# Seven half-width block products in the second FFN, with GpSimd making the operand sums

## The reference, cut to what matters

```python
def swiglu(h, w_gate, w_up, w_down):
    return (jax.nn.silu(h @ w_gate) * (h @ w_up)) @ w_down

x = x + g2 * swiglu(modulate(x, norm_ffn_g[l], sh2, sc2), ffn_w_gate[l], ffn_w_up[l], ffn_w_down[l])
```

## Time and profile before

| | |
|---|---|
| time, median of 3 | 1623.81 us (1623.81 to 1623.95) |
| the profiled execution | 1622.71 us |
| its span | 1620.9 us |
| TensorE busy | 1583.2 us, 98% |
| VectorE busy | 991.5 us, 61% |
| ScalarE busy | 647.5 us, 40% |
| GpSimd busy | 133.7 us, 8% |

### The profile page before, as it was taken

How to read it: one execution, slowest core, us unless ns; L and a number is a source line. 1 busy time by engine, 2 the same in 40 slices (tenths; PEclk the granted TensorE clock), 3 DMA queues, 4 the chain that set the end, 5 groups by cost and what they waited for, 6 DMA issues and landing times.

```text
span 1620.9 us, 25828 instructions
## 1 busy us (share of the span) xinstructions
PE 1583.2 (98%) x10032; PEld 1362.1 (84%) x10032; DVE 991.5 (61%) x1547; ACT 647.5 (40%) x1187; POOL 133.7 (8%) x183
## 2 busy tenths in 40 slices
PE   6999999999999999999999999999999999999999
PEld 5887777678799899899989977888887888888887
DVE  4798888543896388368638666877665533333334
ACT  4444454442743144124214343556683322322222
POOL 0434353010000000000000100100110000000000
PEclk9999999999999999999999999999999999999999
DMA  9633400651113321422231431111135233232332
GB/s 366 73 98 105 144 27 27 231 212 65 66 53 120 115 77 48 164 77 79 104 132 63 149 105 53 53 40 40 66 136 184 78 108 117 91 128 92 116 105 104
DMA packets 49491, 170.48 MB, mean 105 GB/s; under 512 B 5584, under 2 KB 5840, under 8 KB 49264
## 3 DMA queue, kind: packets, MB, share of 16 engines
q1 hardware_dynamic: 37104, 127.00, 22.9%
q10 hardware_dynamic: 7984, 28.31, 4.9%
q0 software_dynamic: 4304, 13.80, 2.9%
HBM read 164.87 MB, written 4.19 MB: 104 GB/s over the span
## 4 chain that ended last, share of the span: by engine, by line
PE 91%; DVE 4%; ACT 3%; issue 1%; DMA 0%; ACTq 0%; SPq 0%; DVEq 0%
PE PS L711 39%; PE PS L2776 9%; PE PS L2557 8%; PE PS L2400 6%; PE PS L2404 6%; PE PS L2401 6%; PE PS L2511 1%; PE PS L2471 1%; PE PS L2362 1%; DVE c_early L1868 1%; PE PS L2624 1%; PE PS L2862 1%; PE PS L2605 1%; PE PS L2863 1%; PE PS L2523 1%
## 5 line engine op out<-in xcount | busy, mean ns | idle before, releaser
L675 DVE TENSOR_TENSOR w_lo<-raw,w_hi 128x1024 fp32r<-128x1024 f32 (+2 forms) x172 | 192.2, 1117 | 128.4 <-ACT w_hi L669 125.2
L669 ACT ACTIVATE w_hi<-raw 128x1024 fp32r<-128x1024 f32 (+2 forms) x172 | 165.4, 962 | 221.4 <-PE PS L711 156.9
L711 PE MATMUL PS<-c_hi,w_hi 128*128 128x512 f32 (+1 forms) x672 | 203.4, 357 | 1.0 <-DVE c_lo L1585 0.6
L711 PE MATMUL PS<-c_lo,w_hi 128*128 128x512 f32 (+1 forms) x672 | 202.0, 354 | 0.0
L1560 DVE SCALAR_TENSOR_TENSOR X<-PS,mod,X 128x512 f32<-128x512 f32 (+2 forms) x120 | 75.7, 658 | 198.2 <-PE PS L711 191.8
L711 PE MATMUL PS<-c_hi,w_lo 128*128 128x512 f32 (+1 forms) x672 | 152.0, 355 | 0.0
L711 PE MATMUL PS<-h_hi,w_hi 128*128 128x512 f32 x368 | 139.2, 385 | 0.9 <-ACT scr L903 0.6
L711 PE MATMUL PS<-h_lo,w_hi 128*128 128x512 f32 x368 | 139.0, 385 | 0.0
L1868 DVE SCALAR_TENSOR_TENSOR c_early<-X,small,c_early 128x798 f32<-128x798 f32 x120 | 134.0, 1116 | 2.9
L711 PEld LDWEIGHTS PS<-c_hi,w_hi 128*128 128x128 f32 x672 | 110.7, 188 | 21.0 <-issue 1.2
L711 PEld LDWEIGHTS PS<-c_lo,w_hi 128*128 128x128 f32 x672 | 110.4, 188 | 18.6
(11 more groups left out here) (405 smaller groups left out, 3080.1 us busy)
## 6 DMA issues: line engine op xcount, KB each, us to landing
raw<-in_w SPq DMA_DIRECT2D x152, 512.0 KB, 3.3
adaw<-in_ada ACTq DMA_DIRECT2D x28, 512.0 KB, 4.3
adaw<-in_w SPq DMA_DIRECT2D x20, 512.0 KB, 4.1
scr<-in_ada POOLq DMA_DIRECT2D x19, 512.0 KB, 9.1
raw<-in_w SPq DMA_DIRECT2D x24, 384.0 KB, 3.1
h_early<-in_ada SPq DMA_DIRECT2D x12, 512.0 KB, 6.2
scr<-in_ada ACTq DMA_DIRECT2D x12, 512.0 KB, 6.8
scr<-in_ada SPq DMA_DIRECT2D x4, 1024.0 KB, 14.3
```

What stands on the lines that cost most here:

```text
L669: nc.scalar.activation(w_hi[:, j, 0:tiles], raw[:, j].rearrange("p (k n) -> p k n", k=KT)[:, 0:tiles], ACT.Copy).then_inc(s_hi, 1)
L675: nc.vector.tensor_tensor(w_lo[:, j, 0:tiles], raw[:, j].rearrange("p (k n) -> p k n", k=KT)[:, 0:tiles], w_hi[:, j, 0:tiles].bitcast(f32) ...
L711: last = nc.tensor.matmul(G[j][:, a:b], w[:, j, k], m[:, k, a:b], start=(n == 1), stop=(n == 3 * k_tiles))
```

## The change

Of the second FFN's 22 gate/up pairs, 20 are now made by seven block products of 12 matmuls with 256 columns each, 84 in place of 48 with 512. The numbers 1 to 7 name the products. Four points differ from the first FFN:

- **Chained PSUM.** A pair uses three banks. 1, 6, 7 and 4 add up in one bank, 5 and 3 in the second, 2 has the third. Before 6 is added, ScalarE copies 1 out (`copied_1`); before 7, the sum so far (`copied_u2`); before 3, product 5 (`copied_5`). VectorE reads the bank after 7 (`up_1`) before 4 is added. Two pairs alternate between banks 0 to 2 and 5 to 7.
- **Seven weight slots.** Each product has its own slot for `hi` and `lo` (two lie in unused columns of `c_hi` and `c_lo`).
- **GpSimd** makes the four sums of a pair's weights (four 128x512 operations, called op 1 to op 4 here) and one of the four sums of inputs. Op 3 overwrites the block of product 1 and so waits for its `lo`.
- **Order.** TensorE takes 1, 5, then 4 of the pair before, then 6, 3, 2, 7. At a group's end the first down slice begins before product 4 of the last pair and goes on after it.

During the norm ScalarE also writes `h_whole` (8 more operations of 128x512). SyncE loads a pair's two 128x1024 chunks into `raw` or `adaw` in turn. The first FFN and all else stay as they were.

GpSimd's list:

```diff
+            for q in range(NB, 2 * NB):
+                a0, a1, u0, u1 = (four(chunk(q, c)[:, n:n + 512]) for c in range(2) for n in (0, 512))
+                for c in range(2):
+                    pool.wait_ge(s_pw[q % 2][c], 16 * (q // 2) + 16)
+                if q >= NB + 2:
+                    pool.wait_ge(s_bl, 7 * (q - 2) + SPLIT_AT[7])
+                nc.gpsimd.tensor_tensor(SUM_7[q % 2], a0, u0, ALU.subtract).then_inc(s_sb, 1)
+                pool.wait_ge(s_sb, 4 * q + 1)
+                nc.gpsimd.tensor_tensor(u0, u0, u1, ALU.add).then_inc(s_sb, 1)
+                pool.wait_ge(s_sb, 4 * q + 2)
+                pool.wait_ge(s_bl, 7 * q + SPLIT_AT[1])
+                nc.gpsimd.tensor_tensor(a0, u0, a0, ALU.subtract).then_inc(s_sb, 1)
+                pool.wait_ge(s_sb, 4 * q + 3)
+                if q >= NB + 2:
+                    pool.wait_ge(s_bl, 7 * (q - 2) + SPLIT_AT[3])
+                nc.gpsimd.tensor_tensor(SUM_3[q % 2], a1, a0, ALU.subtract).then_inc(s_sb, 1)
```

ScalarE's, for the pairs of a group:

```diff
+                    for q in range(first, end):
+                        last = q + 1 == end
+                        copied_1(q)
+                        stream_hi(act, q, 6)
+                        copied_5(q)
+                        stream_hi(act, q, 3)
+                        if q == NB:
+                            act.wait_ge(s_gf[1], half + 1)
+                            hidden_hi(1)
+                            sum_hi(3)
+                        stream_hi(act, q, 2)
+                        copied_u2(q)
+                        stream_hi(act, q, 7)
+                        if q > first:
+                            pair_hi(q - 1, q - 1 + tile)
+                        stream_hi(act, q, 4)
+                        silu_1(q)
+                        if not last:
+                            stream_hi(act, q + 1, 1)
+                        else:
+                            act.wait_ge(s_bp, BLOCK_AT[q, 5])
+                            split_hi(act, R // 2, 0, tiles=nf)
+                        silu_0(q)
+                        if not last:
+                            stream_hi(act, q + 1, 5)
+                    pair_hi(q, q + tile)
```

VectorE's:

```diff
+                    for q in range(first, end):
+                        last = q + 1 == end
+                        if q > first:
+                            up_1(q - 1)
+                            gated_1(q - 1)
+                        stream_lo(dve, q, 6)
+                        stream_lo(dve, q, 3)
+                        if q == NB:
+                            hidden_lo(1, 1)
+                            sum_lo(2)
+                        if q > first:
+                            gated_0(q - 1)
+                        stream_lo(dve, q, 2)
+                        stream_lo(dve, q, 7)
+                        if q > first:
+                            hidden_lo(q - 1 + tile, q - 1 + tile - f0)
+                        stream_lo(dve, q, 4)
+                        gate_1(q)
+                        if q == NB:
+                            sum_lo(3)
+                        if not last:
+                            stream_lo(dve, q + 1, 1)
+                        else:
+                            split_lo(dve, R // 2, 0, tiles=nf)
+                        gate_0(q)
+                        if not last:
+                            stream_lo(dve, q + 1, 5)
+                    up_1(q)
+                    gated_1(q)
+                    gated_0(q)
+                    hidden_lo(q + tile, q + tile - f0)
```

TensorE's (a bank's product also waits for the bank's readers, which is cut here):

```diff
+            def stream_block(q, b):
+                pe.wait_ge(s_bh, 7 * q + SPLIT_AT[b])
...
+                for k in range(4):
+                    MM(chained(q, b), w_h[:, k], m_h[:, k], start=(opens and k == 0), stop=False, skip_group_check=not opens)
+                    MM(chained(q, b), w_h[:, k], m_l[:, k], start=False, stop=False, skip_group_check=not opens)
+                pe.wait_ge(s_bl, 7 * q + SPLIT_AT[b])
+                for k in range(4):
+                    last = MM(chained(q, b), w_l[:, k], m_h[:, k], start=False, stop=(k == 3), skip_group_check=not opens)
+                last.then_inc(s_bp, 1)
...
+                for g, (f0, nf) in enumerate(GROUPS):
-                    with pe.Fori(1 if g == 0 else 0, nf) as i:
-                        half = pe.snap(i + R // 2)
-                        product(pe, half, 0, h_hi, h_lo, ONLY)
-                        product(pe, half, 1, h_hi, h_lo, ONLY)
+                    for q in range(first, end):
+                        stream_block(q, 1)
+                        stream_block(q, 5)
+                        if q > first:
+                            stream_block(q - 1, 4)
+                        for b in (6, 3, 2, 7):
+                            stream_block(q, b)
...
+                    pe.wait_ge(s_hid, hid - 1)
+                    for k in range(nf - 1):
+                        down_pass(k, w_hi, c_hi, nf)
+                        down_pass(k, w_hi, c_lo, nf)
+                    stream_block(end - 1, 4)
+                    pe.wait_ge(s_lo, R + 1)
+                    for k in range(nf - 1):
+                        down_pass(k, w_lo, c_hi, nf)
+                    pe.wait_ge(s_hid, hid)
+                    down_pass(nf - 1, w_hi, c_hi, nf)
+                    down_pass(nf - 1, w_hi, c_lo, nf)
+                    down_pass(nf - 1, w_lo, c_hi, nf).then_inc(s_gemm, 1)
```

More of the change, by code:

```diff
@@ L49, with block_stream @@
 R_F1 = R_O1 + 8
-NP = R_F1 + 2 * FT + 32
-NR = NP + 2 * (FT - PLAIN)
+NP = R_F1 + 2 * PLAIN + 32
+NB = FT - PLAIN
+NR = NP + 4 * NB
+def block_stream():
+    at, n = {}, 7 * NB
+    for f, end in zip(FIRST, PAIRS):
+        for q in range(NB + f, NB + end):
+            for b in (1, 5, 4, 6, 3, 2, 7):
+                if b != 4 or q > NB + f:
+                    n += 1
+                    at[q - (b == 4), b] = n
+        n += 1
+        at[NB + end - 1, 4] = n
+    return at
+BLOCK_AT = block_stream()
+SPLIT_AT = {1: 1, 5: 2, 6: 3, 3: 4, 2: 5, 7: 6, 4: 7}
 SM = {}
@@ L1003, in ffn, with gate_silu @@
             def ffn():
-                R = R_F1
-                def hidden(half, i):
+                R, half = R_F1, R_F1 // 2 + 1
+                def gate_silu(half):
                     act.wait_ge(s_gemm, 2 * half + 1)
@@ L1010, in hidden, with hidden_hi @@
                     nc.scalar.activation(sg[:, 0:LAT], G[0][:, 0:LAT], ACT.Silu).then_inc(s_gf[0], 1)
[L1011 to L1014, removed]
[L1016 to L1023 removed]
+                def hidden_hi(at):
+                    nc.scalar.activation(c_hi[:, at, 0:LAT], ftmp[:, 0:LAT], ACT.Copy).then_inc(s_hhi, 1)
@@ new lines, in silu_1, with pair_hi @@
+                def silu_1(q):
+                    act.wait_ge(s_g1s, q + 1)
+                    nc.scalar.activation(sg[:, LH:LAT], sg[:, LH:LAT], ACT.Silu).then_inc(s_s1, 1)
+                def pair_hi(q, at):
+                    act.wait_ge(s_f, 2 * q + 2)
+                    hidden_hi(at)
+                split_hi(act, half, 0)
+                act.wait_ge(s_nwh, 24)
+                gate_silu(half - 1)
+                act.wait_ge(s_gf[1], half)
+                hidden_hi(0)
+                split_hi(act, half, 1)
@@ new lines, in ffn @@
+                sum_hi(0)
+                gate_silu(half)
+                stream_hi(act, NB, 1)
+                sum_hi(1)
+                stream_hi(act, NB, 5)
+                sum_hi(2)
+                R += 2 * PLAIN
+                for g, (f0, nf) in enumerate(GROUPS):
+                    first, end = NB + FIRST[g], NB + PAIRS[g]
+                    tile = PLAIN - f0 - NB
+                    for q in range(first, end):
[17 more added lines that the diff above has]
+                            stream_hi(act, q + 1, 1)
+                        else:
+                            act.wait_ge(s_bp, BLOCK_AT[q, 5])
+                            split_hi(act, R // 2, 0, tiles=nf)
[3 more added lines that the diff above has]
+                    pair_hi(q, q + tile)
+                    act.wait_ge(s_bp, BLOCK_AT[q, 2])
@@ L1766, in hidden, with hidden_lo @@
                     V.tensor_tensor(ftmp[:, 0:LAT], G[1][:, 0:LAT], sg[:, 0:LAT], ALU.mult).then_inc(s_gf[1], 1)
[L1767 to L1770, removed]
-                dve.wait_ge(s_mod, 28)
-                for g, (f0, nf) in enumerate(GROUPS):
[L1774 to L1781, removed]
+                def hidden_lo(f, at):
+                    dve.wait_ge(s_hhi, FT + f + 1)
+                    V.tensor_tensor(c_lo[:, at, 0:LAT], ftmp[:, 0:LAT], c_hi[:, at, 0:LAT].bitcast(f32), ALU.subtract)\
+                        .then_inc(s_hid, 1)
```

221 lines of the change are left out of this document (196 added, 25 removed).

## The result

| | before | after |
|---|---|---|
| median of 5 runs | 1623.95 us (1623.81 to 1624.57) | 1642.27 us (1639.72 to 1644.74) |
| ratio, 95% interval | 1 | 1.0113 [1.0102, 1.0124] |
| profiled execution, its span | 1622.71, 1620.9 us | 1643.15, 1641.3 us |

What follows compares the result with a forecast made beforehand. TensorE's matmul time was taken to bound the second FFN. Groups 211.3, products 4 5.8, groups' ends 6.0 and start 1.5 make 224.6, minus 217.8 removed: 6.8 more than 1623.8, so 1630.6 us, range 1617 to 1637.

Steps and rivals of the forecast that it cites:

- Removed work: Second FFN, TensorE: 20 pairs of 48 matmuls at 0.2269 us go away, 217.8 us.
- the product's price: TensorE: matmuls of 256 columns start 0.12 us apart, so a block takes 1.44 us and a pair 10.08.
- The loop: Steady pair: block 5 waits for hi 5, behind silu_0, which waits for gate_0 behind lo 1; 10.84 us a pair.
- the forecast's own sign: TensorE's waits should fall on block 5; if block 1 waits instead, the loop's bound was misplaced.
- The shared port: GpSimd's sums and VectorE's SBUF operations take turns, each meeting costing VectorE 0.84 us; 11.25 a pair, bounds 10.84 and 11.37.
- that branch: Steady pair: lo 5 comes before op 4, later sums meet lo 6, lo 3 and lo 2; 11.14 us a pair.
- The first stretches: Each group, start to block 6 of its second pair: ten blocks, 14.4 us, plus about 0.35 for collisions.
- The groups' ends: Down stage: waits for the last hidden tile, 0.9 us and a restart, 1.3 in the last group; 6.0 together.
- The signs: TensorE's second-FFN waits rise to about 25 us, mostly block 5's hi and lo; met lo splits read 1.3 to 1.6.
- TensorE the bound: Rival, second FFN: TensorE stays the bound, 10.2 us less, 1613.6; with half of it near 1619; chance 0.20 for both.
- The loop alone: Rival, second FFN: the loop without port collisions, 10.84 us a pair, 1624.4 us, no change; chance 0.22.
- a second operation of GpSimd falls on the loop: Rival, steady pair: op 1 and op 2 reach lo 7 to lo 4; about 11.8 us a pair, 1638; chance 0.08.

Runs made afterwards that it cites:

- e4: The changed kernel with the four GpSimd weight sums moved to VectorE, hi 1 ahead of silu_1 and hi 5 ahead of silu_0: 1611.2 us, ratio 0.9917.
- e1: The changed kernel with each of GpSimd's four weight sums cut to 128x8 elements, order and semaphores kept: 1624.0 us, ratio 0.9992 to the kernel before.
- e7: e4 with the passes for c_lo that stood ahead of product 4 at group ends moved behind it: 1608.4 us, ratio 0.9906 to the kernel before.
- e3: The changed kernel with GpSimd's four sums cut to 128x8 elements, hi 5 ahead of silu_0 and lo 5 ahead of gate_0: 1614.3 us, ratio 0.9936.
- e2: The changed kernel with hi 5 ahead of silu_0 on ScalarE and lo 5 ahead of gate_0 on VectorE, sums whole: 1632.3 us, ratio 1.0047.
- e9: e4 with the weight sums back on GpSimd, its order of hi 1, hi 5 and the silus kept: 1620.1 us, ratio 0.9976 to the kernel before.
- e5: The changed kernel with op 1 and op 2 cut to 128x8 elements, op 3 and op 4 whole: 1624.9 us, ratio 0.9994 to the kernel before.

## Why the prediction was wrong, step by step

- **Removed work, and the product's price.** Right. Blocks lie 0.12 us a matmul apart, and with nothing to wait for (e4) a pair takes 10.00 us where 10.08 stood. By the Trainium skill ("TensorE: Matmul & The Clock Gate", section "Wait — 56ns, not 53.3ns?") it would be 9.2, an estimate from its 0.109 us a matmul. The trace of e4, where TensorE doesn't wait in a steady pair, shows 10.0.
- **The loop.** Right: block 5 behind hi 5 behind `silu_0` behind `gate_0`, block 1 to block 5 in 2.03 us (2.03 forecast), 10.80 a pair with the sums out of the way (10.84 forecast). The extended durations held: 0.42, 0.42, 0.39. By the forecast's own sign, a wait at block 1, the bound of the changed kernel was misplaced all the same; the next point says how.
- **The shared port: the step that failed.** The mechanism was right. The failed sentences are "op 4 and the next pair's op 1 and op 2 slide into the stretch of lo 6, lo 3 and lo 2, and lo 7 starts some 0.3 late: 11.14" and, in the sum, 11.25. Lo 5 did come first, as that branch has it, by 0.17 us (1410.53 against op 4 at 1410.70), with lo 5 0.8 later than worked out and op 4 1.1: that this branch came true is partly luck. Two sizes were off. The operations were costed at 1.02 each from a pair in which one operand is a single value per partition, spread over the row (L607); on two whole tensors one takes 1.29 alone and 1.48 to 1.68 in a collision, so the row of four lasts 6.2 us. And three VectorE instructions in a row are held up, by 0.57 + 1.09 + 1.09 = 2.75 us, against a slack of 1.91 (e1), where the forecast priced a meeting at 0.84 and never added up the three. Lo 7 was late by 0.8, not 0.3, and the bound moved off TensorE: a pair is then a loop of VectorE and ScalarE alone, 11.64. Twelve loops: 3.8 us.
- **The first stretches: the same error, twice as dear.** "About 0.35 for the same collision (0 to 0.65)" measured 2.0 (16.44 against 14.45 in e1, three times), and 2.9 in the first group (18.91 against 16.01), some 0.5 of which is the lower clock of the last section: block 5 began at 1296.55 though its hi was ready at 1295.97. At a group's start GpSimd does two pairs' sums in a row, from 1361.35 on in the trace, and meets lo 6, lo 3 and lo 2 with op 4, op 1 and op 2, as the first rows of the two timelines show. Blocks 6, 3 and 2 wait 0.18 each for their low halves, blocks 1 and 5 of the second pair 0.5 each, and each of the five has a restart of 0.1: 2.0 together. This and the first group's extra are 7.7 us of the 11.1 that were missing. I looked at the first stretch with the steady pair's eyes, though op 1 and op 2 of two pairs fall together there.
- **The groups' ends.** Right: waits of 3.4 us for `c_lo`, the longest 1.2 (forecast 0.9 three times and 1.3).
- **The signs.** TensorE's waits came to some 18 us, not 25, none of them for the `lo` of block 5, and met splits read up to 1.78 us where 1.3 to 1.6 was foretold.
- **Rivals.** TensorE the bound: e4 and e7 show what it would have taken, other lists and sums off GpSimd; even e3 stands at 10.20. The loop alone is what e1 shows. The rival "a second operation of GpSimd falls on the loop" (0.08, 11.8 a pair, 1638) was nearest, with one difference: op 1 and op 2 needn't reach lo 7 themselves; what they push in front of it is enough. Its condition, operations on two whole tensors costing well over 1.02, had been written down and put aside for the cheaper row.

The Trainium skill ("SBUF — State Buffer", section "Who interferes with whom") says that a VectorE instruction with two SBUF inputs contends with a GpSimd one that reads SBUF, and calls the shared port pair an exclusive lock. The traces agree: a VectorE instruction caught in a meeting ends 0.55 (512 columns) or 0.28 (256) behind GpSimd's, each time.

## What to carry to other kernels

When an idle engine takes over work, cost what it does to the engine that shares a resource with it before what it spares it: count the meetings in the order in which they come, add up what all of them cost it, and only then take off its slack ahead of the first instruction on the critical loop. Do it again for the first round of each loop, where the helper has several rounds' work at once. And in lists that run in order, put what the bounding engine waits for ahead of what merely waits for that engine: two entries moved were worth 0.6 us a pair, and made lateness elsewhere cheap.

## What the runs showed of the hardware

- GpSimd's 128x512 subtraction or addition on two whole tensors takes 1.29 us alone; with one operand spread from a single value per partition, two take 2.04. A row of the same size and another operand layout was not a fair price.
- VectorE's 128x512 split in a collision took 1.11 to 1.82 us for 0.69 (all traces here), and GpSimd's operation 1.47 to 1.78, once 2.16, for 1.29 (the changed kernel's): both lose.
- In a meeting each instruction ends a fixed time after the other engine's: VectorE's 0.55 us behind with 512 columns and 0.28 with 256, whatever its duration reads (1.11 to 1.82); GpSimd's 1.15 behind in a row of turns. So a meeting can be priced by counting turns.
- The granted clock fell twice in the profiled execution of the changed kernel. Stretch, then PE, PEld, DVE, ACT, POOL busy, clock, DMA share, GB/s:

```profile
971.00:974.00 3.00, 2.92 (x12) 1.99 (x11) 2.40 (x5) 1.84 (x4) 0.00 (x0) 0.68 0.00 0
974.00:978.00 4.00, 4.00 (x15) 3.52 (x15) 2.38 (x5) 1.03 (x3) 0.00 (x0) 0.50 0.43 131
...
1289.40:1291.50 2.10, 0.36 (x4) 0.15 (x2) 2.10 (x4) 0.33 (x1) 0.00 (x0) 1.00 0.01 4
1291.50:1292.90 1.40, 1.40 (x12) 1.40 (x13) 1.40 (x4) 0.00 (x0) 0.00 (x0) 1.00 0.43 47
1292.90:1296.30 3.40, 3.40 (x18) 3.22 (x17) 2.40 (x5) 1.87 (x4) 1.41 (x2) 0.51 0.76 287
```

From 1292.9 to 1296.3 TensorE ran at the lower level of 1.2 GHz, after the wait of 1.7 us for a late lo 2, which the row of 1289.40 shows as 0.36 us busy of 2.10, and after 1.4 us of full work. From the first to the last of eight matmuls there it is 1.66 us instead of 0.83. That the wait was the cause isn't shown, and the wait alone is not enough: e2 and e9 have a wait of 1.7 us at the same block, and their clock stays at 1.00 from 1290 to 1300 us. The fall at 971 to 978 lies ahead of all that was changed. In the trace of before the clock is 1.00 there, with 25 matmuls from 974 to 978 us where the row here has 15. It accounts for most of the 2.5 us by which the spans differ outside of the second FFN. It isn't the change's: e1 and e5 have the same fall, and e2, with the changed kernel's whole work, has none. Why one execution has it and another hasn't stays open.
